# Which PSUM bank the first projections after a seam are written to

## The reference

```
for l in range(DEPTH):
    h = rms_norm(x, g[0])
    ...                                   # projections of h, the mixer
    x = x + rms_norm(mix, g[1])           # mix = (...) @ w_out
    h = rms_norm(x, g[2])
    hid = causal_dwconv(h @ w_up, conv_w, conv_b)
    gate, val = jnp.split(hid, 2, axis=-1)
    x = x + rms_norm((gelu(gate) * val) @ w_down, g[3])
```

## Time and profile before

| | us |
|---|---|
| median of 3 runs | 1612.28 |
| lowest, highest | 1612.06, 1612.81 |
| the profiled execution's own time | 1611.24 |
| its span | 1609.5 |
| TensorE busy with matmuls | 1564.4 |
| VectorE busy | 1067.6 |
| ScalarE busy | 834.1 |
| GpSimd busy | 155.9 |

### The profile page before, as it was taken

How to read it: one execution, slowest core, us unless ns; L and a number is a source line. 1 busy time by engine, 2 the same in 40 slices (tenths; PEclk the granted TensorE clock), 3 DMA queues, 4 the chain that set the end, 5 groups by cost and what they waited for, 6 DMA issues and landing times.

```text
span 1609.5 us, 23497 instructions
## 1 busy us (share of the span) xinstructions
PE 1564.4 (97%) x9140; PEld 1337.4 (83%) x9140; DVE 1067.6 (66%) x1981; ACT 834.1 (52%) x1526; POOL 155.9 (10%) x150
## 2 busy tenths in 40 slices
PE   8999999999999999999999999999999999999998
PEld 7978999879878888878888877887888888888887
DVE  7688777786777877765693657416647865555665
ACT  6876555555666556452213456533336364646564
POOL 0110111110000304100000001000003000000000
PEclk9999999999999999999999999999999999999999
DMA  7566665565355545542111111114322333333233
GB/s 264 173 242 206 229 223 197 183 210 171 108 207 194 181 152 183 180 136 92 53 40 66 53 53 40 66 66 147 111 96 95 116 106 115 106 105 107 90 121 128
DMA packets 61886, 217.70 MB, mean 135 GB/s; under 512 B 7888, under 2 KB 8144, under 8 KB 61648
## 3 DMA queue, kind: packets, MB, share of 16 engines
q1 hardware_dynamic: 60784, 214.53, 39.5%
q10 hardware_dynamic: 992, 1.67, 0.4%
HBM read 215.09 MB, written 1.05 MB: 134 GB/s over the span
## 4 chain that ended last, share of the span: by engine, by line
PE 68%; DVE 12%; issue 9%; ACT 8%; POOL 2%; DMA 0%; DVEq 0%; SPq 0%; POOLq 0%; ACTq 0%
PE PS L357 19%; PE PS L359 18%; PE PS L358 18%; DVE WL L324 3%; PE PS L2862 3%; ACT WH L307 2%; POOL AR L1647 2%; PE PS L2172 2%; PE PS L2237 1%; PE PS L515 1%; PE PS L2214 1%; DVE X L488 1%; PE PS L1991 1%; PE PS L2892 1%; ACT AR L1791 1%
## 5 line engine op out<-in xcount | busy, mean ns | idle before, releaser
L324 DVE TENSOR_TENSOR WL<-RAWB,WH 128x1024 fp32r<-128x1024 f32 x345 | 424.7, 1234 | 226.1 <-ACT WH L307 220.3
L357 PE MATMUL PS<-RH,WH 128*128 128x256 f32 (+1 forms) x1560 | 497.1, 319 | 8.0 <-DVE RH L539 3.0
L358 PE MATMUL PS<-RH,WH 128*128 128x256 f32 (+1 forms) x1560 | 490.0, 314 | 0.0
L359 PE MATMUL PS<-RH,WL 128*128 128x256 f32 (+1 forms) x1560 | 489.9, 314 | 0.0
L307 ACT CAST WH<-RAWB 128x1024 fp32r<-128x1024 f32 x346 | 359.5, 1042 | 206.0 <-PE PS L359 197.8
L357 PEld LDWEIGHTS PS<-RH,WH 128*128 128x128 f32 x1560 | 298.0, 191 | 34.2 <-issue 6.1
L358 PEld LDWEIGHTS PS<-RH,WH 128*128 128x128 f32 x1560 | 298.1, 191 | 18.2 <-issue 0.2
L359 PEld LDWEIGHTS PS<-RH,WL 128*128 128x128 f32 x1560 | 297.8, 191 | 18.0
L357 PE MATMUL PS<-WH,RH 128*128 128x512 f32 (+1 forms) x768 | 303.7, 395 | 5.8 <-ACT WH L307 1.3
L358 PE MATMUL PS<-WL,RH 128*128 128x512 f32 (+1 forms) x768 | 296.3, 386 | 0.0
L359 PE MATMUL PS<-WH,RH 128*128 128x512 f32 (+1 forms) x768 | 295.9, 385 | 0.0
(11 more groups left out here) (374 smaller groups left out, 1655.9 us busy)
## 6 DMA issues: line engine op xcount, KB each, us to landing
RAWB<-ws SPq DMA_DIRECT2D x370, 512.0 KB, 3.5
AR<-ws SPq DMA_DIRECT2D x20, 512.0 KB, 4.8
X<-ws SPq DMA_DIRECT2D x4, 512.0 KB, 5.4
TMP<-gains SPq DMA_DIRECT2D x8, 256.0 KB, 4.3
CS<-cs SPq DMA_DIRECT2D x1, 1472.0 KB, 7.9
X<-x SPq DMA_DIRECT2D x2, 512.0 KB, 4.0
AR<-dec ACTq DMA_DIRECT2D x2, 512.0 KB, 6.6
X<-ctx SPq DMA_DIRECT2D x2, 512.0 KB, 7.1
```

Of the source, the lines that this page charges most:

```text
L324: eng.e.tensor_tensor(k.WL[:, i % SPL, :], k.RAWB[:, i % RAW, :], k.WH[:, i % SPL, :].bitcast(F32), ALU.subtract).then_inc(*eng.done("wl", i))
L357: pe.e.matmul(o, wh, xh, start=first, stop=False)
L358: pe.e.matmul(o, wh, xl, start=False, stop=False)
L359: return pe.e.matmul(o, wl, xh, start=False, stop=last)
```

## The change

At the end of the four seams with modulation sums, the two banks of block 1 are put on a list `ahead`, and the next two calls of `take` get these two in order, without moving the ring's counter. Everything after them is taken in turn as before, from where the counter stands. No instruction is added or taken out on any engine, but for the waits that go with a bank.

```diff
@@ class Ring
         self.tiles, self.n, self.holder, self.place, self.freed, self.held = tiles, 0, {}, {}, {}, set()
+        self.ahead = []
 
     def take(self, eng, *name):
-        while self.n % len(self.tiles) in self.held:
+        if self.ahead:
+            i = self.ahead.pop(0)
+        else:
+            while self.n % len(self.tiles) in self.held:
+                self.n += 1
+            i = self.n % len(self.tiles)
             self.n += 1
-        i = self.n % len(self.tiles)
-        self.n += 1
         if i in self.holder:
             for sem, value in self.freed.get(self.holder[i], {}).values():
                 eng.wait_ge(sem, value)
@@
+    def drop_to_front(self, *names):
+
+        for name in names:
+            self.held.discard(self.place[name])
+        self.ahead += [self.place[name] for name in names]
@@ def seam_pe(k, pe, m)
     if banks:
-        for h in range(2):
-            k.ps.drop(m.s, "out", 1, h)
+        k.ps.drop_to_front((m.s, "out", 1, 0), (m.s, "out", 1, 1))
```

## The result

| | before | after |
|---|---|---|
| median (20 runs before, 19 after) | 1612.69 us | 1615.19 us |
| lowest of them | 1610.91 us | 1611.80 us |
| the profiled execution's own time, its span | 1611.24, 1609.5 us | 1615.0, 1613.3 us |

The changed kernel takes 1.0016 times as long, with a 95% interval of 1.0010 to 1.0023: 2.6 us slower, where 0.70 us less was predicted. A twentieth run of the changed kernel took 6744.78 us and is in neither the median nor the ratio. The predicted 1611.6 was for a kernel before at 1612.28; over more runs that one stands at 1612.69. The difference of 0.4 us is not the miss; the sign is.

A forecast was written before the change was run, and what follows sets the result against it. TensorE, busy for 97% of the span, was taken as the bound, so only its idle time counts. Terms -0.66 (ffn0) and -0.04 (fox) gave -0.70 us, from 1612.28 to 1611.6 us; range 1610.4 to 1613.2.

The forecast's parts named there:

- The bank and the ring: At ffn0 and fox TensorE waits for the next PSUM bank in turn, not the operand; ffn1 and even2 have no such wait.
- the pace of the tiles: At ffn0 the first projection's tiles follow VectorE's low parts, one per 0.416 us, 0.63 us behind.
- ffn0, -0.66 us: ffn0's second projection, bound by VectorE's WL, starts at 136.60 in place of 137.26: gain 0.66 us, bounds 0 and 1.48.
- So the 0.66 us are carried through: After ffn0's second projection TensorE has no wait until the stage's end, so the whole 0.66 us is kept.
- fox, -0.04 us: At fox the turning of the modulation sums waits for VectorE's copy: gain 0.04 us, bounds -0.02 and 0.08.
- The wait of 1.48 us: TensorE's wait between turning X and the first projection, in ffn0 and fox; in fox it moves behind the first product.
- The short way round the ring: Fox's second value product gets its bank just in time, cost 0; as rival, a cast later, +1.05 us, 1612.6, chance 0.06.
- The added waits. Cost 0: Later products at the four seams reuse the two banks sooner; their readers finish in time, so these waits cost 0.
- No DMA is added: In the whole kernel the change adds no DMA; those that follow TensorE start earlier with it.
- the same waits as before: A sign of the prediction: at ffn1 and even2 the timeline shows unchanged waits.
- The rivals: Whole wait goes, 1609.3, 0.05; nothing kept, 1612.3, 0.12; clock falls, 1613.1, 0.07; short way round costs, 1612.6, 0.06.
- clock rival: Small steps of the first projection at ffn0 and fox drop TensorE's clock: 0.86 us slower, 1613.1 us, chance 0.07.

The follow-up runs named there:

- r7: Kernel before with 9 idle waiting instructions on TensorE between fox's and ffn1's seams, no bank moved; ratio 1.0016 to the kernel before.
- r1: The kernel before, unchanged, run again as a control; median 1612.66 us, ratio 0.9999 to the kernel before.
- r2: Kernel before with the new bank order at the seams ahead of ffn0 and fox alone; median 1614.52 us, ratio 1.0007.
- r6: Kernel before with ffn0's banks alone changed and 4 idle waiting instructions on TensorE between fox's and ffn1's seams; ratio 1.0010.
- r12: The changed kernel once more, all four seams with the new bank order, against the kernel before; ratio 1.0016.
- r11: Kernel before with fox's banks alone changed, no idle instructions, a repeat; ratio 0.9998.
- r9: Kernel before with ffn0's banks alone changed and 94 idle waiting instructions on TensorE between fox's and ffn1's seams; ratio 0.9994.
- r13: Repeat of the kernel with ffn0's banks alone changed and 94 idle waiting instructions; median 1612.50 us, ratio 0.9996 to the kernel before.

## Why the prediction was wrong

**The bank and the ring: right.** The two seams where the change acts, the two where it doesn't, and the pace of the tiles came as counted.

**ffn0, -0.66 us: right at the seam, 0.57 at the stage's end.** From the second turn to the second projection all nine profiled executions with ffn0's banks changed take 5.83 or 5.84 us, and all seven without take 6.49 or 6.50. To the first turn of fox's seam the nine take 196.25 to 196.27 us and the seven 196.82 to 196.84. "So the 0.66 us are carried through" missed the 0.09 us by which the second projection is longer when it begins with a wait.

**fox, -0.04 us: right within its bounds of -0.02 and 0.08.** It is 0.07 us: 6.43 or 6.44 us in the seven with the change, 6.49 to 6.51 in the nine without; where the clock did not fall, 0.03 us of it are left at ffn1's seam. The wait of 1.48 us moved behind the first product, where it is 1.05. The short way round the ring did not cost anything.

**"The added waits. Cost 0": the step that failed.** I priced each wait by when it is fulfilled, and on that count 0 is right: none of them holds TensorE. I did not price it as an instruction. "No DMA is added" failed with it: the number of fetches stayed at 73, but 9 more instructions placed one of them 4.6 us earlier (from +3.68 to -0.93), among the loads on which the seam waits. By the ratio of r7 this costs 2.6 us (1.1 to 4.0), by its median 2.4, which outweighs the 0.60 us that the two seams keep. That the ffn1 seam would have "the same waits as before" was wrong for the same reason.

**The size of it.** At the seam itself the gap of the second turn grows by 0.8 to 1.3 us. From the first turn to the start of the second projection the five kernels with the fetch among the loads take 1.58 us more in the mean than the profile of before (1.22 to 1.79), the ten others 0.09 (-0.81 to 0.77; the slower turning behind the gap and the clock are in it). That is 1.5 us. It stays: from ffn1's first turn to even2's the five take 233.23 to 233.81 us and the eleven others 231.22 to 232.81, 1.5 us apart in the mean. What r7 has beyond this, to 2.6, I cannot place: its interval begins at 1.1, so it need not be there.

**Sum of the parts.** By the recorded ratios ffn0 alone gives 0.9993, fox alone 1.0003 and 0.9998, the other two seams 1.0000, nine instructions 1.0016. The product is 1.0007 to 1.0012, against 1.0016 measured twice, with an uncertainty of 0.0007 to 0.0009 in each of them. The parts account for the sign, and for the size within what these measurements can tell.

**The rivals.** None was this one. The fall of the clock was nearest to it. At ffn0, where the small steps of the first projection begin, the granted clock of the changed kernel was 1.00 throughout; the first number behind the counts:

```profile
130.00:140.00 10.00, 9.29 (x80) 8.50 (x73) 9.67 (x19) 7.98 (x14) 0.00 (x0) 1.00 0.38 122
```

With that, the rule of the prediction's clock rival, that many short pauses between groups of matmuls can make the clock swing (Trainium skill, page "TensorE: Matmul & The Clock Gate", section "A second HAM failure mode: psum-queue depth-cycling"), finds nothing at ffn0; at fox the three falls of seven are open between it and chance.

**The noise.** The range was drawn from three runs within 0.75 us. Its upper end of 1613.2 did not follow its own rule either: the slowest case it takes in, 1613.1, with 0.4 us for the runs is 1613.5. The measured 1615.19 lies above both. Over 20 runs the kernel before goes from 1610.91 to 1615.27. The profile of before was one of its quick executions as well: in r1, the same kernel, the clock fell once more, from 980.9 us on, and that cost 1.6 us. A sum of tenths on one profile was sharper than either could bear.

## What to carry to other kernels

An instruction added to a full engine's program need not be only its own wait: it can move later fetches of that program, and a fetch that comes to lie among the loads on which a seam hangs can cost more than a small saving brings. It need not: five more instructions moved nothing here, and at even2's seam a fetch among the loads went with a gap as short as without one in four profiles. So before crediting or blaming an edit of under 0.2%, add a few idle instructions to the kernel before, and see how far its time moves by that alone; and look in the DMA queues for the packets of kind "instruction" beside the transfer that is late. Where one is found, move it by further idle instructions before the edit itself is given up.

## What the runs showed of the hardware

- TensorE's program came in 73 packets of 16384 bytes, one for each 256 instruction records. In the kernel before they took 0.88 to 2.05 us each, 39 of them 1.0 us or less; among ffn1's weight loads it was 0.96 to 1.71 us.
- The place of a fetch does not move evenly with the instructions ahead of it. With 0, 4 and 5 more it began 3.64 to 3.82 us behind ffn1's first turn, with 9 more 0.53 to 1.28 us ahead of it, with 99 more 5.53 to 5.85 us ahead. By place in the program the nine shifted it by far more than nine: it began when TensorE had started 6653 to 6658 of its records with 0 to 5 more, and 6569 to 6596 with 9 more. What starts a fetch no run shows.
- One packet of 16 KB delayed a chunk of 512 KB by 1.1 to 1.6 us (landing at 2.45 to 2.94 and not 1.27 to 1.61 us). That is much more than its share of 16 engines (3.6% of 3 us, 0.1 us), but near the 0.96 to 1.71 us for which it held the one engine that carried it; that the chunk waits for its part on that engine is possible and not shown. In r2, r6 and after, SyncE's last of the four issues took 1.4 to 2.0 us where it takes 0.4; in r7 and r12 it took 0.5, and the chunk was late all the same. By which way the fetch delays the loads is open. At even2's seam a fetch stood among the loads in all kernels but those with 99 more. There SyncE's second issue took 1.1 to 1.7 us in all eleven and 0.37 us in the five others. The gap was 2.06 to 2.48 us in the eleven (2.06 in r2, r7, r11 and r12) and 2.06 or 2.07 us in the five: this fetch did not always cost.
- TensorE's clock went to half for 3.4 us at places that differ from one execution to the next of the same kernel (between 930 and 990 us: at 960.4 us in the changed kernel, nowhere in r12, which is the same; at 979.3 in r9 and 936.3 in r13), at 1.6 to 1.7 us each. At ffn1's second turn, behind the same gap of 2.00 us, it fell in most profiles but not in r9 and r11, where that turn took 2.05 us.
